# SiLU of the delta heads written through tanh, in three parts, with VectorE multiplying

## The chip, the core and the metric

The kernel runs on one core of a Trainium2 chip. TensorE does the matmuls, VectorE, ScalarE and GpSimd the elementwise work, each engine in the order of its own program; they wait for each other on semaphores. ScalarE computes functions such as Exp, Ln, SiLU or Tanh from a table set that must be loaded first; a load shows in its program as ACT_TABLE_LOAD. The metric is the device time of one execution in microseconds, as a median over runs.

## What is computed

Two blocks of a small transformer over 272 tokens (16 meta tokens and 256 others) of width 1024. The change lies in the first layer, in the mixer that joins a gated delta rule of four heads with a window attention of eight. Of the delta part this matters here:

```python
qkv = jax.nn.silu(centred_conv(jnp.concatenate([hq, hk, hv], axis=-1), conv_w))
q, k, v = split_cols(qkv, (A_QKW, A_QKW, A_VW))          # 512 columns each: 4 heads of 128
q = l2norm(q.reshape(bsz, n, A_HEADS, A_DK)) * (A_DK ** -0.5)
k = l2norm(k.reshape(bsz, n, A_HEADS, A_DK))             # x * rsqrt(sum(x * x) + EPS)
v = v.reshape(bsz, n, A_HEADS, A_DV)
```

silu(x) is x * sigmoid(x), which equals 0.5 * x * (1 + tanh(x / 2)).

## The kernel before

Activations are held with the model's columns on the 128 partitions and the 272 tokens (T) along the free axis. `qkv` is 12 such chunks of 272: queries 0 to 3, keys 4 to 7, values 8 to 11. Weights are split into a high and a low part (`w_hi` by ScalarE at L1771, `w_lo` by VectorE at L2511), so that three matmuls of TensorE (L675) give one product; 24 of them make a tile of the projection.

The stretch in question is one loop of ten steps, k = 0 to 9, that each of the engines runs in its own program. It interleaves three things. First the projection's 16 tiles (`qkvz_tile` on TensorE, `qkvz_step` on VectorE at L2879, which takes a tile from its bank; `next_split` on ScalarE). Second the convolution of the twelve chunks: ScalarE makes products (`conv_products`, L2122), GpSimd the others and the sums (L3592, L3595), and VectorE does chunk 11 alone (`last_conv`, L2850 and L2852); `conv_done` and `conv_last` tell that they are finished. Third the window attention in nine units: TensorE's scores (L1381, L1386), VectorE's bias and maximum (`window_logits`, L2910 to L2925), ScalarE's exponents (`window_exponents`, L2075), VectorE's reciprocal and scaling (`window_normalise`, L2932, L2935), TensorE's transposes (`window_turn`, L1399 to L1403), ScalarE's copies (`window_copies`, L2085 to L2089), TensorE's product with the values (`window_values`, L1412, L1415, and L1421 for unit 8), ScalarE's copy of the result (`window_result`, L2097) and VectorE's low part of it (`window_low`, L2526).

Into the end of this loop the delta heads are woven. In step 6 ScalarE, once the convolution is done, takes the SiLU of all of `qkv` in place (L2156) and then has the table set with logarithm and exponential loaded again (`log_and_exp`, L2011). In step 7 it squares keys and queries (L2150). In step 8 TensorE sums the squares over each head with a matmul by ones (`delta_sum`, L1435), ScalarE takes the logarithm of the sums and the exponential of minus half of it (`delta_logs`, L2108, L2111), and VectorE multiplies the heads by it (`delta_norm`, L2963), keys first, then queries. Behind the loop TensorE transposes values and then keys into token order (`delta_turn`, L1451), ScalarE copies them out (L2163), and the delta rule itself begins (`gated_delta`, L963 and on). GpSimd, when the convolution is done and the projection is read, fills the identity tiles of the delta rule (`identity_tiles`, L3605, L3606).

All orders are written out by hand; each engine's place in the loop is the order of the code in its own program.

Of the kernel before, what the change touches and what calls it, by code (L numbers as in the profile page):

```python
# [25 lines left out]
ALU, ACT, AX = mybir.AluOpType, mybir.ActivationFunctionType, mybir.AxisListType  # L26

P = 128
# [3 lines left out]
T = NMETA + SEQ  # L32
# [174 lines left out]
def program(nc, w, out):  # L207
# [3 lines left out]
    with ExitStack() as ctx:  # L211
# [23 lines left out]
        work = sb("work", [P, 2656])  # L235
# [70 lines left out]
        for d in range(2):  # L306
# [73 lines left out]
        dve_step, act_step, pool_step, out_sent = sem("dve_step"), sem("act_step"), sem("pool_step"), sem("out_sent")  # L380

        M = {n: sem(n) for n in (
            "ab_turned ab_turn_read conv_given conv_done conv_last d_blocks d_copied d_cum d_cum_read d_diff d_dm d_egr d_first d_gate_exp d_gates d_gk d_kdec "
            "d_kn d_kq d_ln d_n d_nn d_o1 d_o d_o_read d_qe d_rows d_s d_s_kept d_s_read d_tiles d_turned d_v d_vnew d_w d_w_copied d_wk "
            "d_wk_copied d_x d_x5 d_x6 d_xt d_y d_yt f_ready f_t f_w f_w_copied f_x f_xt f_y "
            "q_meta sink_meta d_sq d_qsum d_rs d_normed g_ln g_mixed g_n g_read g_sq g_stat gelu kv_dup l_att l_attc l_e1 l_exp l_gate l_ks "
# [100 lines left out]

            return conv_four[:, c // 2 % 2, j - 1] if given_taps(c) == 5 else conv_pair[:, c // 2 % 2]

        KEYS, QUERIES = 0, 1  # L490
        delta_sq = {KEYS: area(work, 0, 4, T), QUERIES: area(mx, 9952, 4, T)}
        delta_r = {KEYS: area(work, 4 * T, 4, T), QUERIES: area(mx, 9952 + 4 * T, 4, T)}
        delta_heads = {KEYS: qkv[:, 4:8], QUERIES: qkv[:, 0:4]}


        PREPARED = CHAINS[0:2] + FIRST + CHAINS[2:]
# [163 lines left out]
        def _(pe):  # L660
# [780 lines left out]
            def delta_turn(i, m, source):  # L1441

                s, e = TILES[m]
                if source == 4:
                    pe.wait_ge(M["d_normed"], 1)
                else:
                    pe.wait_ge(M["d_ln"], 2)
                if i >= 4:
                    pe.wait_ge(M["d_copied"], i - 3)
                for h in range(A_HEADS):  # L1450
                    mm = pe.transpose(tile_bank[i % 4][0:e - s, h * P:(h + 1) * P], qkv[:, source + h, s:e], ident)  # L1451
                mm.then_inc(M["d_turned"], 1)
# [300 lines left out]
        def _(act):  # L1753
# [255 lines left out]
            def log_and_exp():  # L2009

                nc.scalar.preload_act_table_set("natural_log_exp_and_others")  # L2011
# [104 lines left out]
            def conv_products(c):  # L2116
# [6 lines left out]
                                         scale=col("conv", 12 * j + c))  # L2123
                ins.then_inc(M["conv_given"], 1)

            for k in range(WINDOW_UNITS + 1):
                if k == 0:
                    next_split(1)
                if k < 6:
                    conv_products(2 * k)  # L2130
                if k < WINDOW_UNITS:
                    window_exponents(k)
                if k < 6:
                    next_split(2 * k + 2)
                if k == 2:
                    act.wait_ge(M["d_cum_read"], 1)
                    act.activation(necc[0:NMETA, 0], gcc[0:NMETA, 0], ACT.Exp)
                    act.activation(necc[:, 1:3], gcc[:, 1:3], ACT.Exp).then_inc(M["d_gate_exp"], 1)
                if k == 8:
                    delta_logs(KEYS)  # L2140
                if k >= 1:
                    window_result(k - 1)
                if k < 6:
                    next_split(2 * k + 3)
                if k < 5:
                    conv_products(2 * k + 1)
                if k == 7:
                    act.wait_ge(M["silu_done"], 1)
                    for which in (KEYS, QUERIES):
                        act.activation(delta_sq[which], delta_heads[which], ACT.Square).then_inc(M["d_sq"], 1)  # L2150
                if k < WINDOW_UNITS:
                    window_copies(k)
                if k == 6:
                    act.wait_ge(M["conv_done"], 11)
                    act.wait_ge(M["conv_last"], 1)
                    act.activation(qkv, qkv, ACT.Silu).then_inc(M["silu_done"], 1)  # L2156
                    log_and_exp()
                if k == 8:
                    delta_logs(QUERIES)
            for i, (m, source) in enumerate(delta_turns()):  # L2160
                n = TILES[m][1] - TILES[m][0]
                act.wait_ge(M["d_turned"], i + 1)
                act.activation((v_tok if source == 8 else k_tok)[0:n, m], tile_bank[i % 4][0:n, 0:4 * P].rearrange(  # L2163
                    "p (h d) -> p h d", h=4), ACT.Copy).then_inc(M["d_copied"], 1)

            def decays(chain):

# [325 lines left out]
        def _(dve):  # L2493
# [465 lines left out]
            def delta_norm(which):  # L2959

                heads = delta_heads[which].rearrange("p h t -> p (h t)")
                dve.wait_ge(M["d_rs"], which + 1)
                dve.scalar_tensor_tensor(heads, heads, P ** -0.5 if which == QUERIES else 1.0,  # L2963
                                         delta_r[which].rearrange("p h t -> p (h t)"), ALU.mult, ALU.mult)\
                    .then_inc(M["d_normed"], 1)

            dve.wait_ge(M["sink_meta"], 1)
            for k in range(WINDOW_UNITS + 1):
# [17 lines left out]
                    delta_gates()  # L2986
                if k == 5:
                    last_conv()
                if k == 8:
                    delta_norm(QUERIES)  # L2990
            dve.wait_ge(M["d_cum_read"], 1)
# [559 lines left out]
        def _(pool):  # L3551
# [69 lines left out]
                    .then_inc(done, 1)  # L3621

            pool.wait_ge(M["conv_done"], 11)
            pool.wait_ge(tile_read, tile_at[phases["ab_qkvz"].first] + 16)
            for chain in CHAINS:
                identity_tiles(chain)
# [64 lines left out]
```

## Time and profile before

| | us |
|---|---|
| median of three runs | 1565.97 |
| lowest | 1565.91 |
| the profiled execution, whole | 1562.62 |
| its span on the core, first to last instruction | 1560.8 |
| TensorE busy (matmuls) | 1520.3 |
| VectorE busy | 1099.1 |
| ScalarE busy | 798.1 |
| GpSimd busy | 173.7 |

The mean granted clock of TensorE in the profiled execution was 0.994 of its full speed. Times in the rows further down are microseconds from the start of the span. An engine's timeline gives for each merged group of instructions its start, its length, the line, operation, tiles and count, and in brackets how long the engine was idle before it and which instruction ended that. The chain of work that ended last is read from the last instruction backwards, each time to what released it.

### The profile page before, as it was taken

Reading aid. Unit: us, or ns where it says so; the run is one execution under the profiler, and the core shown is the slowest. Engines: PE = TensorE matmul, PEld = TensorE weight load, DVE = VectorE, ACT = ScalarE, POOL = GpSimd, SP = SyncE. Lnnn points to the kernel's source line nnn. Section 1 sums busy time; section 2 is a strip of 40 time slices with the busy share of each in tenths; the row PEclk is TensorE's granted clock in tenths of the full one; section 3 lists DMA queues with packets and bytes.
Section 4 is the critical chain, followed back from the end, with each engine's and each line's share of the span. In section 5 each row is a group of like instructions: output and inputs, shape, how many; then the busy total and the mean of one; then the engine's idle time right before and its main releaser. Section 6 shows DMA issues by size and latency. Waiting matters only on the chain.

```text
span 1560.8 us, 31984 instructions
## 1 busy us (share of the span) xinstructions
PE 1520.3 (97%) x12908; PEld 1471.7 (94%) x12908; DVE 1099.1 (70%) x1965; ACT 798.1 (51%) x1369; POOL 173.7 (11%) x187
## 2 busy tenths in 40 slices
PE   6988999999999999999999999999999999999997
PEld 5977899999998999999998999999999999999997
DVE  5784758676778677778778667776668666666666
ACT  4766445343455544446545655444555556554443
POOL 2481203000021200002000201000010010200000
PEclk9998999999999999999999999999999999999999
DMA  6420016454441345454433424656444444356561
GB/s 223 163 109 1 3 55 213 174 184 180 162 162 68 109 169 208 162 202 176 163 137 134 166 101 141 216 165 209 168 162 163 162 164 161 109 176 202 166 210 58
DMA packets 124791, 236.35 MB, mean 151 GB/s; under 512 B 2614, under 2 KB 50025, under 8 KB 124665
## 3 DMA queue, kind: packets, MB, share of 16 engines
q1 hardware_dynamic: 123177, 230.24, 42.2%
q0 software_dynamic: 1296, 4.28, 0.9%
q8 instruction: 91, 1.49, 0.4%
q14 instruction: 35, 0.29, 0.1%
q10 hardware_dynamic: 192, 0.05, 0.0%
HBM read 233.51 MB, written 1.05 MB: 150 GB/s over the span
## 4 chain that ended last, share of the span: by engine, by line
PE 88%; DVE 6%; ACT 2%; issue 2%; POOL 1%; DMA 0%; ACTq 0%; DVEq 0%; POOLq 0%
PE ps L675 49%; PE ps L722 6%; PE ps L721 6%; PE ps L720 6%; PE ps L683 6%; PE ps L844 2%; DVE w_lo L2511 2%; PE ps L821 1%; PE ps L771 1%; PE ps L806 1%; DVE hidden L2562 1%; PE ps L831 1%; POOL square_sum L3567 0%; DVE chain_memory L3124 0%; ACT w_hi L1771 0%
## 5 line engine op out<-in xcount | busy, mean ns | idle before, releaser
L1771 ACT ACTIVATE w_hi<-raw 128x1024 fp32r<-128x1024 f32 x440 | 460.6, 1051 | 282.1 <-PE ps L722 135.3
L2511 DVE TENSOR_TENSOR w_lo<-raw,w_hi 128x1024 fp32r<-128x1024 f32 x440 | 547.0, 1243 | 9.4 <-ACT w_hi L1771 9.1
L675 PE MATMUL ps<-u_hi,w_hi 128*128 128x256 f32 (+1 forms) x1464 | 422.6, 289 | 1.9 <-issue 1.2
L675 PE MATMUL ps<-u_hi,w_lo 128*128 128x256 f32 (+1 forms) x1464 | 416.8, 285 | 0.0
L675 PE MATMUL ps<-u_lo,w_hi 128*128 128x256 f32 (+1 forms) x1464 | 416.3, 284 | 0.0
L675 PEld LDWEIGHTS ps<-u_hi,w_hi 128*128 128x128 f32 x1464 | 278.0, 190 | 8.0 <-issue 5.6
L675 PEld LDWEIGHTS ps<-u_hi,w_lo 128*128 128x128 f32 x1464 | 278.1, 190 | 0.0
L675 PEld LDWEIGHTS ps<-u_lo,w_hi 128*128 128x128 f32 x1464 | 277.0, 189 | 0.6
L675 PE MATMUL ps<-a_hi,w_hi 128*128 128x256 f32 x800 | 226.7, 283 | 0.6 <-DVE hidden L2562 0.3
L675 PE MATMUL ps<-a_lo,w_hi 128*128 128x256 f32 x800 | 224.9, 281 | 0.0
L675 PE MATMUL ps<-a_hi,w_lo 128*128 128x256 f32 x800 | 224.8, 281 | 0.0
L722 PE MATMUL ps<-a_hi,w_lo 128*128 128x256 f32 (+1 forms) x720 | 204.9, 285 | 0.0
L721 PE MATMUL ps<-a_lo,w_hi 128*128 128x256 f32 (+1 forms) x720 | 204.5, 284 | 0.0
L720 PE MATMUL ps<-a_hi,w_hi 128*128 128x256 f32 (+1 forms) x720 | 204.5, 284 | 0.0
L2562 DVE TENSOR_TENSOR hidden<-ps,hidden 128x256 f32<-128x256 f32 (+1 forms) x272 | 115.7, 425 | 101.7 <-PE ps L722 59.4
L2550 DVE TENSOR_TENSOR work<-ps,rs 128x256 f32<-128x256 f32 (+1 forms) x153 | 65.4, 427 | 133.9 <-PE ps L675 118.0
L675 PEld LDWEIGHTS ps<-a_hi,w_hi 128*128 128x128 f32 x800 | 151.1, 189 | 2.2 <-DVE w_lo L2511 0.8
L675 PEld LDWEIGHTS ps<-a_hi,w_lo 128*128 128x128 f32 x800 | 151.3, 189 | 0.0
L675 PEld LDWEIGHTS ps<-a_lo,w_hi 128*128 128x128 f32 x800 | 150.4, 188 | 0.1
L720 PEld LDWEIGHTS ps<-a_hi,w_hi 128*128 128x128 f32 x720 | 135.8, 189 | 0.2 <-DVE a_lo L2526 0.2
L722 PEld LDWEIGHTS ps<-a_hi,w_lo 128*128 128x128 f32 x720 | 136.0, 189 | 0.0
L721 PEld LDWEIGHTS ps<-a_lo,w_hi 128*128 128x128 f32 x720 | 135.4, 188 | 0.0
(469 smaller groups left out, 2257.1 us busy)
## 6 DMA issues: line engine op xcount, KB each, us to landing
raw<-in_w_ff_dram SPq DMA_DIRECT2D x32, 2048.0 KB, 7.7
raw<-in_ffn_w_gu_dram SPq DMA_DIRECT2D x44, 1024.0 KB, 6.9
raw<-in_ffn_w_down_dram SPq DMA_DIRECT2D x10, 2048.0 KB, 8.0
raw<-in_xa_w_kv_dram SPq DMA_DIRECT2D x8, 2048.0 KB, 8.3
raw<-in_od_w_in_dram SPq DMA_DIRECT2D x6, 2048.0 KB, 7.8
raw<-in_w_in_ab_dram SPq DMA_DIRECT2D x5, 2048.0 KB, 7.9
raw<-in_ev_w_in_dram SPq DMA_DIRECT2D x5, 2048.0 KB, 7.8
raw<-in_xa_w_q_dram SPq DMA_DIRECT2D x4, 2048.0 KB, 7.6
```

Of the source, the lines that this page charges most:

```text
L675: mm = pe.matmul(bank[:, 0:n], wx[:, q, k * P:(k + 1) * P], x[ux][:, k, ts], start=k == 0 and i == 0, stop=k == KD - 1 and i == 2)
L683: mm = pe.matmul(bank[:, at:at + n_quarters * n].rearrange("p (q n) -> p q n", n=n), x[ux][:, k, ts], wx[:, q:q + n_quarters, k * P:k * P ...
L720: pe.matmul(tile_bank[t % 4][:, 0:n], hi[:, k, cols], a[0][:, at_k, ts], start=k == 0, stop=False)
L721: pe.matmul(tile_bank[t % 4][:, 0:n], hi[:, k, cols], a[1][:, at_k, ts], start=False, stop=False)
L722: mm = pe.matmul(tile_bank[t % 4][:, 0:n], lo[:, k, cols], a[0][:, at_k, ts], start=False, stop=k == chunks - 1)
L771: mm = pe.matmul(banks[u_ % 2][:, 0:n], matrix, hn_sq[:, u_ % 2, i * n:(i + 1) * n], start=i == 0, stop=i == tiles - 1)
L806: mm = pe.matmul(bank[:, column:column + matrix.shape[1]], part, matrix, start=i == 0, stop=i == len(parts) - 1)
L844: mm = pe.matmul(bank[x["parts"], r * P:r * P + x["nq"]], vs[r], at_pt[0:rows, v % 2, c, 0:x["nq"]], start=c == 0, stop=c == len(x["keys"] ...
L1771: act.activation(quarter(w_hi, b, q), raw_quarter(b, q), ACT.Copy).then_inc(high_split, 1)
L2511: dve.tensor_tensor(quarter(w_lo, b, q), raw_quarter(b, q), quarter(w_hi, b, q).bitcast(F32), ALU.subtract)\
L2550: dve.tensor_tensor(target, tile_bank[t][:, 0:n], rs[:, ts] if scale is None else scale, ALU.mult)\
L2562: dve.tensor_tensor(hidden[:, k, ts], tile_bank[t][:, 0:ts.stop - ts.start], hidden[:, k, ts], ALU.add)\
```

## The change

The table set that holds Exp and Tanh is loaded ahead of the loop. In step 6 ScalarE takes, in place of the SiLU, tanh(x / 2) of keys, queries and values, in three activations, into areas of their own. VectorE multiplies (tanh + 1) by x, for keys and queries at the end of its step 7, for values in its step 8 between `window_low` and the scaling of the queries; this is twice the SiLU. The squares take 0.5 as scale, the scalings of keys and queries and the copies of the transposed values a factor of 0.5. The squares of keys wait for the first product, those of queries for the second; behind them, and ahead of `window_copies(7)`, stands the load of the set with logarithm and exponential. The transposes on TensorE and the tile filling on GpSimd wait for the third product too.

```diff
--- before.py
+++ after.py
@@ -487,10 +487,11 @@
 
             return conv_four[:, c // 2 % 2, j - 1] if given_taps(c) == 5 else conv_pair[:, c // 2 % 2]
 
-        KEYS, QUERIES = 0, 1
+        KEYS, QUERIES, VALUE_HEADS = 0, 1, 2
         delta_sq = {KEYS: area(work, 0, 4, T), QUERIES: area(mx, 9952, 4, T)}
         delta_r = {KEYS: area(work, 4 * T, 4, T), QUERIES: area(mx, 9952 + 4 * T, 4, T)}
-        delta_heads = {KEYS: qkv[:, 4:8], QUERIES: qkv[:, 0:4]}
+        delta_heads = {KEYS: qkv[:, 4:8], QUERIES: qkv[:, 0:4], VALUE_HEADS: qkv[:, 8:12]}
+        delta_tanh = {KEYS: area(work, 4 * T, 4, T), QUERIES: area(mx, 9952 + 4 * T, 4, T), VALUE_HEADS: area(mx, 9952 + 8 * T, 4, T)}
 
 
         PREPARED = CHAINS[0:2] + FIRST + CHAINS[2:]
@@ -1445,6 +1446,7 @@
                     pe.wait_ge(M["d_normed"], 1)
                 else:
                     pe.wait_ge(M["d_ln"], 2)
+                    pe.wait_ge(M["silu_done"], 3)
                 if i >= 4:
                     pe.wait_ge(M["d_copied"], i - 3)
                 for h in range(A_HEADS):
@@ -2123,6 +2125,7 @@
                                          scale=col("conv", 12 * j + c))
                 ins.then_inc(M["conv_given"], 1)
 
+            nc.scalar.preload_act_table_set("exp_and_others")
             for k in range(WINDOW_UNITS + 1):
                 if k == 0:
                     next_split(1)
@@ -2145,23 +2148,24 @@
                 if k < 5:
                     conv_products(2 * k + 1)
                 if k == 7:
-                    act.wait_ge(M["silu_done"], 1)
                     for which in (KEYS, QUERIES):
-                        act.activation(delta_sq[which], delta_heads[which], ACT.Square).then_inc(M["d_sq"], 1)
+                        act.wait_ge(M["silu_done"], which + 1)
+                        act.activation(delta_sq[which], delta_heads[which], ACT.Square, scale=0.5).then_inc(M["d_sq"], 1)
+                    log_and_exp()
                 if k < WINDOW_UNITS:
                     window_copies(k)
                 if k == 6:
                     act.wait_ge(M["conv_done"], 11)
                     act.wait_ge(M["conv_last"], 1)
-                    act.activation(qkv, qkv, ACT.Silu).then_inc(M["silu_done"], 1)
-                    log_and_exp()
+                    for which in (KEYS, QUERIES, VALUE_HEADS):
+                        act.activation(delta_tanh[which], delta_heads[which], ACT.Tanh, scale=0.5).then_inc(M["delta_tanh"], 1)
                 if k == 8:
                     delta_logs(QUERIES)
             for i, (m, source) in enumerate(delta_turns()):
                 n = TILES[m][1] - TILES[m][0]
                 act.wait_ge(M["d_turned"], i + 1)
                 act.activation((v_tok if source == 8 else k_tok)[0:n, m], tile_bank[i % 4][0:n, 0:4 * P].rearrange(
-                    "p (h d) -> p h d", h=4), ACT.Copy).then_inc(M["d_copied"], 1)
+                    "p (h d) -> p h d", h=4), ACT.Copy, scale=0.5 if source == 8 else 1.0).then_inc(M["d_copied"], 1)
 
             def decays(chain):
 
@@ -2960,9 +2964,15 @@
 
                 heads = delta_heads[which].rearrange("p h t -> p (h t)")
                 dve.wait_ge(M["d_rs"], which + 1)
-                dve.scalar_tensor_tensor(heads, heads, P ** -0.5 if which == QUERIES else 1.0,
+                dve.scalar_tensor_tensor(heads, heads, 0.5 * P ** -0.5 if which == QUERIES else 0.5,
                                          delta_r[which].rearrange("p h t -> p (h t)"), ALU.mult, ALU.mult)\
                     .then_inc(M["d_normed"], 1)
+
+            def double_silu(which):
+
+                dve.wait_ge(M["delta_tanh"], which + 1)
+                dve.scalar_tensor_tensor(delta_heads[which], delta_tanh[which], 1.0, delta_heads[which], ALU.add, ALU.mult)\
+                    .then_inc(M["silu_done"], 1)
 
             dve.wait_ge(M["sink_meta"], 1)
             for k in range(WINDOW_UNITS + 1):
@@ -2986,6 +2996,11 @@
                     delta_gates()
                 if k == 5:
                     last_conv()
+                if k == 7:
+                    double_silu(KEYS)
+                    double_silu(QUERIES)
+                if k == 8:
+                    double_silu(VALUE_HEADS)
                 if k == 8:
                     delta_norm(QUERIES)
             dve.wait_ge(M["d_cum_read"], 1)
@@ -3621,6 +3636,7 @@
                     .then_inc(done, 1)
 
             pool.wait_ge(M["conv_done"], 11)
+            pool.wait_ge(M["silu_done"], 3)
             pool.wait_ge(tile_read, tile_at[phases["ab_qkvz"].first] + 16)
             for chain in CHAINS:
                 identity_tiles(chain)
```

What stands in the engines' programs. On ScalarE, at the place where the loop begins: the last row of the gates is the one at L2066 (L2068 after), then comes the weights' copy for the projection. Before:

```order
L2065 ACTIVATE small<-small 128x24 [waits act_step]
L2066 ACTIVATE small<-small,cst 128x24 [waits act_step]
L1771 ACTIVATE w_hi<-raw 128x1024 [waits tile_summed]
L2122 ACTIVATE mx<-mx,late 128x272 [waits tile_read]
L2075 ACTIVATE att,small<-att,small 128x273 [waits at_max]
```

On ScalarE at the same place, in the changed kernel (L1773 is the weights' copy, L2124 a convolution product, L2077 the exponents of unit 0):

```order
L2067 ACTIVATE small<-small 128x24 [waits act_step]
L2068 ACTIVATE small<-small,cst 128x24 [waits act_step]
L2128 ACT_TABLE_LOAD
L1773 ACTIVATE w_hi<-raw 128x1024 [waits tile_summed]
L2124 ACTIVATE mx<-mx,late 128x272 [waits tile_read]
L2077 ACTIVATE att,small<-att,small 128x273 [waits at_max]
```

One load more stands there, ahead of everything of the loop.

On ScalarE in steps 6 to 8, from the copies of window unit 6 to the logarithms of the keys (`ps` are the banks, `att` the window's probabilities, `mx` and `work` hold the heads). Before:

```order
L2086 ACTIVATE att<-ps 32x128
L2156 ACT_TABLE_LOAD [waits conv_last]
L2156 ACTIVATE mx<-mx 128x3264 [waits conv_done]
L2011 ACT_TABLE_LOAD
L2075 ACTIVATE att,small<-att,small 128x273 [waits at_prob,at_max]
L2097 ACTIVATE a_hi<-ps 128x128 [waits at_summed]
L2150 ACTIVATE work<-mx 128x1088 [waits silu_done]
L2150 ACTIVATE mx<-mx 128x1088
L2085 ACTIVATE att<-ps 128x512 [waits at_summed,at_turned]
L2108 ACTIVATE work<-ps,cst 128x272 [waits d_qsum]
```

The same stretch of ScalarE in the changed kernel:

```order
L2088 ACTIVATE att<-ps 32x128
L2161 ACTIVATE work<-mx 128x1088 [waits conv_last,conv_done]
L2161 ACTIVATE mx<-mx 128x1088 x2
L2077 ACTIVATE att,small<-att,small 128x273 [waits at_prob,at_max]
L2099 ACTIVATE a_hi<-ps 128x128 [waits at_summed]
L2153 ACTIVATE work<-mx 128x1088 [waits silu_done]
L2153 ACTIVATE mx<-mx 128x1088 [waits silu_done]
L2013 ACT_TABLE_LOAD
L2087 ACTIVATE att<-ps 128x512 [waits at_summed,at_turned]
L2110 ACTIVATE work<-ps,cst 128x272 [waits d_qsum]
```

The two loads around the SiLU are gone, three tanh stand in its place, both squares wait for VectorE, and a load stands between them and the copies of unit 7.

On VectorE in steps 7 and 8, from the tile 15 of the projection (L2879, L2883 after) to the scaling of the queries (L2963, L2967 after). Before:

```order
L2879 TENSOR_TENSOR mx<-ps,rs 128x272 [waits tile_summed]
L2932 RECIPROCAL small<-small 128x2 [waits at_exp]
L2526 TENSOR_TENSOR a_lo<-ps,a_hi 128x128 [waits operand_high]
L2918 COPY att<-small 128x1 [waits at_turned]
L2925 TENSOR_REDUCE small<-att 128x1 [waits at_biased]
L2963 SCALAR_TENSOR_TENSOR mx<-mx,work 128x1088 [waits d_rs]
L2963 SCALAR_TENSOR_TENSOR mx<-mx 128x1088 [waits d_rs]
```

The same stretch of VectorE in the changed kernel:

```order
L2883 TENSOR_TENSOR mx<-ps,rs 128x272 [waits tile_summed]
L2936 RECIPROCAL small<-small 128x2 [waits at_exp]
L2530 TENSOR_TENSOR a_lo<-ps,a_hi 128x128 [waits operand_high]
L2974 SCALAR_TENSOR_TENSOR mx<-work,mx 128x1088 [waits delta_tanh]
L2974 SCALAR_TENSOR_TENSOR mx<-mx 128x1088 [waits delta_tanh]
L2922 COPY att<-small 128x1 [waits at_turned]
L2929 TENSOR_REDUCE small<-att 128x1 [waits at_biased]
L2967 SCALAR_TENSOR_TENSOR mx<-mx,work 128x1088 [waits d_rs]
L2974 SCALAR_TENSOR_TENSOR mx<-mx 128x1088 [waits delta_tanh]
L2967 SCALAR_TENSOR_TENSOR mx<-mx 128x1088 [waits d_rs]
```

Three multiplications (L2974) have come in: two ahead of the logits of unit 8, one ahead of the scaling of the queries.

## Rows read from the trace of the kernel before

**Rows 1.** The page: span, and the engines' shares of the chain that ended last.
```profile
span 1560.8 us, 31984 instructions
...
PE 88%; DVE 6%; ACT 2%; issue 2%; POOL 1%; DMA 0%; ACTq 0%; DVEq 0%; POOLq 0%
```

**Rows 2.** Timeline of ScalarE where the loop begins (start, length, instruction, idle before).
```profile
55.85 1.04 ACT L1771 ACTIVATE w_hi<-raw 128x1024 fp32r<-128x1024 f32 x1
...
57.63 0.51 ACT L2075 ACTIVATE att<-att,small 128x273 f32<-128x273 f32 x1
```

**Rows 3.** Timeline of VectorE in the same stretch.
```profile
58.97 1.15 DVE L2935 TENSOR_SCALAR att<-att,small 128x272 f32<-128x272 f32 x2
```

**Rows 4.** Timeline of TensorE in the same stretch.
```profile
60.01 0.29 PE L675 MATMUL ps<-u_hi,w_lo 128*128 128x272 f32 x1
60.17 0.66 PE L1399 MATMUL ps<-cst,att 128*128 128x128 f32 x4
```

**Rows 5.** Timeline of GpSimd: its first and its last convolution work.
```profile
57.81 0.71 POOL L3592 TENSOR_TENSOR mx<-mx,late 128x272 f32<-128x272 f32 x1 [28.44 <-ACT mx L2122]
...
104.20 10.60 POOL L3595 TENSOR_TENSOR mx<-mx 128x272 f32<-128x272 f32 x10
```

**Rows 6.** The chain in order of time, 60 to 180 us (start, length, what).
```profile
92.94 3.23 PE ps L675 x24
...
114.29 0.95 DVE att L2935 x2
115.28 1.12 PE ps L1399 x4
```

**Rows 7.** Timeline of ScalarE, steps 6 to 8.
```profile
117.41 1.28 ACT L2156 ACT_TABLE_LOAD   x1
118.71 2.93 ACT L2156 ACTIVATE mx<-mx 128x3264 f32<-128x3264 f32 x1
121.65 1.28 ACT L2011 ACT_TABLE_LOAD   x1
122.95 0.52 ACT L2075 ACTIVATE att<-att,small 128x273 f32<-128x273 f32 x1
...
125.14 1.09 ACT L2150 ACTIVATE mx<-mx 128x1088 f32<-128x1088 f32 x1
126.50 0.60 ACT L2085 ACTIVATE att<-ps 128x512 f32<-128x512 f32 x1 [0.27 <-PE ps L1400]
...
130.55 1.62 ACT L2108 ACTIVATE work<-ps,cst 128x272 f32<-128x272 f32 x4 [1.82 <-PE ps L1435]
132.21 1.11 ACT L2111 ACTIVATE work<-work 128x1088 f32<-128x1088 f32 x1
```

**Rows 8.** Timeline of VectorE, steps 7 and 8.
```profile
122.39 0.44 DVE L2879 TENSOR_TENSOR mx<-ps,rs 128x272 f32<-128x272 f32 x1 [2.98 <-PE ps L675]
124.10 0.17 DVE L2932 RECIPROCAL small<-small 128x2 f32<-128x2 f32 x1 [1.27 <-ACT att L2075]
124.30 1.33 DVE L2935 TENSOR_SCALAR att<-att,small 128x272 f32<-128x272 f32 x2
125.56 0.28 DVE L2526 TENSOR_TENSOR a_lo<-ps,a_hi 128x128 fp32r<-128x128 f32 x1
...
133.35 1.29 DVE L2963 SCALAR_TENSOR_TENSOR mx<-mx,work 128x1088 f32<-128x1088 f32 x1 [4.02 <-ACT work L2111]
134.56 0.28 DVE L2526 TENSOR_TENSOR a_lo<-ps,a_hi 128x128 fp32r<-128x128 f32 x1
```

**Rows 9.** Timeline of TensorE: sums of the squared keys, window unit 8.
```profile
127.00 3.52 PE L1435 MATMUL ps<-work,cst 128*128 128x272 f32 x8
...
134.99 2.34 PE L1421 MATMUL ps<-att,mx 16*64 16x32 f32 x24 [0.66 <-DVE a_lo L2526]
```

**Rows 10.** Windows: busy PE, PEld, DVE, ACT, POOL, then PEclk, DMA share, GB/s.
```profile
34.00:36.00 2.00, 1.34 (x9) 1.27 (x10) 0.80 (x1) 1.47 (x5) 0.00 (x0) 1.00 1.04 398
...
128.00:130.00 2.00, 2.00 (x6) 1.35 (x4) 0.61 (x3) 0.61 (x2) 0.00 (x0) 0.50 0.00 0
```

## What I expect of the change, and why

> **What bounds the kernel now.** I read the page's chain of work first: TensorE holds 88% of it in a span of 1560.8 us [rows 1]. The change touches only about 55 to 140 us, so I went to the chain in order of time and to the timelines of single engines there. Between 60 and 96 us the chain is TensorE's projection matmuls (the last piece before it changes hands is at 92.94) [rows 6]. After it the window attention and the convolutions run on ScalarE and VectorE; at 114.29 VectorE normalises the probabilities of unit 6, and TensorE, which stood idle, starts again at 115.28 [rows 6]. From there to 140 us hardly anything overlaps: the chain is a relay. ScalarE loads a table at 117.41, runs the one SiLU at 118.71 for 2.93 us, loads the next table at 121.65 and only at 122.95 gets to the exponents of unit 7 [rows 7]. VectorE normalises them at 124.30 [rows 8]; TensorE sums the squares of the keys from 127.00 [rows 9]; ScalarE takes logarithms at 130.55 and the exponential at 132.21 [rows 7]; VectorE scales the keys at 133.35 and splits unit 7's result at 134.56 [rows 8]; this releases TensorE at 134.99 [rows 9]. Transposes and the delta rule follow. So I forecast by how much 134.99 moves. Behind it all is either relay or TensorE's own work (its 88% of the chain), without slack in which a shift could vanish; I carry it to the end one for one.
>
> **First part: the table load ahead of the window loop.** The new load is the first thing behind the Ln at L2066, so it stands in front of ScalarE's copy of a weight quarter at 55.85, of the first convolution products and of the exponents of unit 0 at 57.63 [rows 2]. All loads of the trace are alike: the one at 121.65 takes 1.28 us, and what follows it starts 1.30 us after it [rows 7]. Neither row lists idle time ahead of it, so ScalarE runs without a gap here [rows 2] and all of it moves by 1.28. Who waits? VectorE's normalising at 58.97 follows the exponents and lasts 1.15, to 60.12 [rows 3]. TensorE's last matmul before it needs these probabilities starts at 60.01, its neighbours are 0.13 apart, and the transposes start at 60.17 [rows 4]. The slack is therefore at most 0.05 us, and TensorE loses about 1.25 us here. I take 1.25. It could be less only if TensorE caught up before 96 us, and there it is the chain itself. A second carrier gives the same: GpSimd gets its first convolution product at 57.81 and then works through to 114.80 (the last ten additions start at 104.20 and last 10.60) [rows 5], so it too ends 1.28 later. That end alone would cost nothing: 116.08 is before 117.41, when the activation behind it could start. An idle stretch of this length doesn't slow TensorE's clock by itself: from 34 to 36 us it was busy 1.34 of 2.00 us at clock 1.00 [rows 10].
>
> **Second part: SiLU replaced by tanh.** Three tanh of 128x1088 take the place of load, SiLU, load. No tanh stands in the trace. From below: the SiLU did 3264 columns in 2.93 us; from above: a single 1088 column activation takes 1.09 (the square at 125.14) [rows 7], so three are 2.93 to 3.27. I take 3.05, nearest to the SiLU, since instructions of one engine overlap at their ends. They start at 117.41 + 1.25 = 118.66, and exponents of unit 7 start at 121.7 instead of 122.95, and end at 122.85 (they took 1.1 us before VectorE went on at 124.10 [rows 8]). So 2.57 us of loads left the place, 1.25 came in early, 0.1 is lost to three instructions: 1.2 us earlier. But VectorE has an earlier duty in its program: it must evacuate projection tile 15, which it did at 122.39 on TensorE's release, in 0.44 us [rows 8]. TensorE is 1.25 late: 123.64, done at 124.08. So the reciprocal of unit 7 stays at about 124.1, where it was. **The gain from the removed loads ends here**: of 1.2 us nothing is left, and tanh has 1.2 us of cover (0.4 each) before it counts.
>
> **Third part: two multiplications and a load in the relay.** The normalising of unit 7 took 1.33 us while GpSimd filled tiles; GpSimd now waits for the third product, so I take the 0.95 of unit 6 [rows 6] and 0.05 around it: from 124.25 to 125.25. The split of window unit 6 (0.28, at 125.56 before [rows 8]) ends at 125.5. Now the new instructions. A multiplication is taken as VectorE's scaling of keys, same operation and shape: 1.29, of which 1.21 until the next starts [rows 8]. Bounds: 1.21 and, with a disturbance as the normalising had, 1.7. Keys 125.45 to 126.7, queries to 127.9. ScalarE squares the keys behind the first (in cover), the queries behind the second, 127.95 to 129.05 (1.09 [rows 7]); then the table load, to 130.3; then what the load was put in front of: the copies of window unit 7, which stood at 126.50 and take 0.60 and a short one [rows 7], to about 131.0; then exponents of unit 8, which are one head, half of the 1.1 above: 131.65. Only then the logarithms of the keys, at 131.7; before, 130.55. TensorE's sum of squared keys starts at 127.8 instead of 127.00 and takes 3.52 at worst [rows 9], to 131.3, so it is no longer the last to arrive. From 131.7 on the relay is the old one: **+1.15 us** on the keys' scaling, the split and TensorE's 134.99.
>
> The rest is in cover. The values' multiplication stands behind the split on VectorE, 135.9 to 137.1, when VectorE formerly waited for the queries' exponential; TensorE needs it only for the transposes of the values, after the 2.3 us of work that 134.99 begins. The squares, with scale 0.5, and the rescaled copies cost what they did. GpSimd's tile filling moves behind the third product, to about 137 us; the delta rule, which reads the tiles, comes behind the transposes.
>
> **A rule against the trace.** The row at 121.65 shows a load that starts when the SiLU ends and is followed by the exponents without a gap [rows 7]. The Trainium skill, ScalarE: Activation LUTs, section What ACT_TABLE_LOAD costs, counts a switch of sets as about 1283 ns of load and about 1380 ns in which the engine drains, 2.66 us in all. The load agrees with this trace; the drain doesn't show in it, so by the row a switch is 1.3.
>
> **Sum.** +1.25 carried in by the first load, -1.3 gained and lost again at tile 15, +1.2 from the third part: relay at 134.99 later by 1.15, say +1.1. Span 1560.8 + 1.1 = 1561.9. The profiled execution took 1562.62; the median of the three times is 1565.97, 3.35 above it, so the median goes to 1567.1.
>
> **Rivals.**
> *The first load is hidden* (TensorE and GpSimd catch up before 115 us, or the exponents of unit 0 were not what it waited for). Then tile 15 comes at 122.39, exponents of unit 7 end at 121.6, and everything of the third part is 1.25 earlier: -0.1 us, 1565.9. For it: both slacks were read from modelled matmul ends. Against: the chain names TensorE without a break up to 96 us [rows 6]. 0.12.
> *TensorE's clock falls less often.* The sums of the keys ran partly at half clock (0.50 from 128 to 130 us) [rows 10], 3.52 us for what at full clock would be no less than half, 1.8. The stretch idle before them becomes shorter. The sums themselves are in cover now, so only work after 134.99 could gain, by perhaps 1.5 us: -0.4, 1565.6. 0.10.
> *Slower: the clock falls once more.* The pause of 1.25 us at 60 us, or a differently cut relay after 125 us, puts a stretch at half clock that wasn't. Price: sums of 3.52 against 1.8 are up to 1.7 us [rows 9]; one or two such stretches on the path give +2.5 to +4.5, 1569. It decides once TensorE shows a clock of 0.50 in a stretch that stood at 1.00 before and that its successor waits for. For it: clock 0.50 [rows 10] in this very place. Against: 1.00 around the pause at 34 us [rows 10]. 0.13.
> *A switch costs more than its row*, twice 1.28: the load ahead of the loop and the one behind the squares both stand on the path, +1.15 + 2.56 = +3.7, 1569.7. Against: the row shows no gap [rows 7]. 0.04. This is the skill's drain, named above; by its figure it would be +3.9.
> *Tanh is slower than 0.4 us above its peers*: +1 to +3. 0.03.
>
> **Chances and range.** Forecast 0.58, its own range 1566 to 1568.5. All cases lie between 1565 and 1570; single executions of before differ by 3.4 us between profile and median, so I open the range to 1562.5 and 1571. A measurement of this kernel can tell some 2%, 31 us, from no change; no mechanism here has a tenth of that. Faster 0.01, within 2% 0.98, slower 0.01.
>
> **What would show it.** Right: the load ahead of the loop lasts 1.28 and TensorE's transposes of unit 0 start near 61.4, waiting for VectorE; tile 15 releases VectorE near 123.6; the reciprocal of unit 7 stays near 124.1; logarithms of the keys near 131.7 follow the exponents of unit 8 at once; the work of 134.99 stands near 136.1. Wrong: transposes of unit 0 at 60.2, or logarithms of the keys waiting for TensorE, or a multiplication over 1.5 us.

## The result, and the profile after

Over 17 executions the changed kernel took 1569.76 us in the median (1565.72 to 1571.66), the kernel before 1564.42 in as many. One execution of the kernel before, a slow one of 1651.88 us, is left out of the ratio. The ratio is 1.0026, with a 95% interval of 1.0018 to 1.0033: some 4 us longer (3 to 5; the medians differ by 5.3), far within 2%. The profiled execution has a span of 1564.1 us against 1560.8 [rows 1], at the same mean clock of 0.994. With 1565.94 us it is one of the fastest five of the changed kernel, so its trace shows 3.3 us and not the whole of a usual execution. The forecast of no visible change, +1.1 us, had the right sign, and less than half of the size.

The traces show four shifts, not one. First the places that the forecast named. ScalarE where the loop begins (start, length, instruction, idle before and what ended it):

```profile
57.87 0.32 ACT L2068 ACTIVATE small<-small,cst 128x24 f32<-128x24 f32 x1
58.20 1.28 ACT L2128 ACT_TABLE_LOAD   x1
59.49 1.06 ACT L1773 ACTIVATE w_hi<-raw 128x1024 fp32r<-128x1024 f32 x1
...
61.28 0.51 ACT L2077 ACTIVATE att<-att,small 128x273 f32<-128x273 f32 x1
```

TensorE of the same kernel, transposes of window unit 0:

```profile
63.76 0.44 PE L1400 MATMUL ps<-cst,att 128*128 128x128 f32 x2 [1.23 <-DVE att L2939]
```

The load takes 1.28 us, and TensorE, which did not idle here before [rows 4], now waits 1.23 us for VectorE. But the weights' copy starts at 59.49, and before it started at 55.85 [rows 2]: 3.64 later, of which the load explains 1.3. Something had already come 2.2 us late before the loop. It is in ScalarE's timeline further ahead. Before:

```profile
40.19 1.06 ACT L1771 ACTIVATE w_hi<-raw 128x1024 fp32r<-128x1024 f32 x1 [3.82 <-DMA raw<-in_w_in_ab_dram]
```

After:

```profile
42.43 1.06 ACT L1773 ACTIVATE w_hi<-raw 128x1024 fp32r<-128x1024 f32 x1 [6.22 <-DMA raw<-in_w_in_ab_dram]
```

A block of projection weights lands 2.24 us later, in a part of the program that the change does not touch.

The relay, ScalarE after, which answers to [rows 7]:

```profile
120.88 1.09 ACT L2161 ACTIVATE work<-mx 128x1088 f32<-128x1088 f32 x1
121.88 2.09 ACT L2161 ACTIVATE mx<-mx 128x1088 f32<-128x1088 f32 x2
123.88 0.51 ACT L2077 ACTIVATE att<-att,small 128x273 f32<-128x273 f32 x1
...
129.90 1.11 ACT L2153 ACTIVATE mx<-mx 128x1088 f32<-128x1088 f32 x1
131.02 1.28 ACT L2013 ACT_TABLE_LOAD   x1
132.32 0.60 ACT L2087 ACTIVATE att<-ps 128x512 f32<-128x512 f32 x1
...
132.97 0.51 ACT L2077 ACTIVATE att<-att,small 128x273 f32<-128x273 f32 x1
...
133.47 1.57 ACT L2110 ACTIVATE work<-ps,cst 128x272 f32<-128x272 f32 x4
```

VectorE after, which answers to [rows 8]:

```profile
125.85 0.44 DVE L2883 TENSOR_TENSOR mx<-ps,rs 128x272 f32<-128x272 f32 x1 [2.86 <-PE ps L676]
126.21 0.15 DVE L2936 RECIPROCAL small<-small 128x2 f32<-128x2 f32 x1
126.40 0.63 DVE L2939 TENSOR_SCALAR att<-att,small 128x272 f32<-128x272 f32 x2
127.17 0.29 DVE L2530 TENSOR_TENSOR a_lo<-ps,a_hi 128x128 fp32r<-128x128 f32 x1
127.38 1.28 DVE L2974 SCALAR_TENSOR_TENSOR mx<-work,mx 128x1088 f32<-128x1088 f32 x1
128.58 1.28 DVE L2974 SCALAR_TENSOR_TENSOR mx<-mx 128x1088 f32<-128x1088 f32 x1
```

TensorE after, which answers to [rows 6] and [rows 9]:

```profile
118.86 1.11 PE L1400 MATMUL ps<-cst,att 128*128 128x128 f32 x4 [5.04 <-DVE att L2939]
...
129.95 2.07 PE L1436 MATMUL ps<-work,cst 128*128 128x272 f32 x8 [1.49 <-ACT work L2153]
...
137.86 2.34 PE L1422 MATMUL ps<-att,mx 16*64 16x32 f32 x24 [0.66 <-DVE a_lo L2530]
140.13 2.79 PE L1453 MATMUL ps<-cst,mx 128*16 128x128 f32 x24
143.79 2.05 PE L964 MATMUL ps<-cst,small 128*128 128x128 f32 x16 [0.88 <-ACT mx L2167]
```

Against before: the transposes of unit 6 are 3.58 later (118.86 for 115.28), the product of unit 8 is 2.87 later (137.86 for 134.99), so the relay itself became 0.71 us shorter. The logarithms follow the exponents of unit 8 with no idle time. Then the clock enters. Before, the transposes of the heads ran in part at half clock; TensorE's rows of before:

```profile
137.26 4.46 PE L1451 MATMUL ps<-cst,mx 128*16 128x128 f32 x24
142.43 2.05 PE L963 MATMUL ps<-cst,small 128*128 128x128 f32 x16 [0.72 <-ACT mx L2163]
```

They took 4.46 us, and 2.79 after; the delta rule starts only 1.36 later than before. This gain is lost again some 45 us later, where the windows of the changed kernel (busy PE, PEld, DVE, ACT, POOL, then granted clock, DMA share, GB/s) show a fall of the clock to 0.50; before it stood at 1.00 in the same work:

```profile
188.00:190.00 2.00, 1.28 (x25) 1.15 (x20) 1.65 (x4) 0.38 (x1) 0.00 (x0) 0.72 0.00 0
190.00:192.00 2.00, 2.00 (x35) 2.00 (x35) 0.29 (x1) 0.66 (x3) 0.00 (x0) 0.50 0.03 8
```

The sum by TensorE's rows: +2.24 (block) +1.34 (load) -0.71 (relay) -1.51 (transposes at full clock) +1.68 (up to 225.03 for 221.99, nearly all of it the fall at 189) = +3.04; the rest up to +3.3 comes in behind.

### The profile page after: what moved, and what is told of

The parts are those of the page before. It is cut to its first block, busy times and chain, and to the rows that moved or that the text cites. A ratio compares the mean times of both kernels' runs of the same rounds, so it can differ in the third digit from the quotient of the medians.

```text
span 1564.1 us, 31992 instructions
## 1 busy us (share of the span) xinstructions
PE 1520.7 (97%) x12908; PEld 1472.4 (94%) x12908; DVE 1102.1 (70%) x1968; ACT 797.1 (51%) x1371; POOL 174.3 (11%) x187
## 4 chain that ended last, share of the span: by engine, by line
PE 87%; DVE 7%; ACT 2%; issue 2%; DMA 1%; POOL 1%; ACTq 0%; DVEq 0%; POOLq 0%
PE ps L676 48%; PE ps L723 6%; PE ps L722 6%; PE ps L721 6%; PE ps L684 6%; PE ps L845 2%; DVE w_lo L2515 2%; PE ps L822 1%; PE ps L772 1%; DMA raw<-in_w_in_ab_dram 1%; PE ps L807 1%; DVE hidden L2566 1%; PE ps L832 1%; POOL square_sum L3582 0%; DVE chain_memory L3139 0%
## 5 line engine op out<-in xcount | busy, mean ns | idle before, releaser
L1773 ACT ACTIVATE w_hi<-raw 128x1024 fp32r<-128x1024 f32 x440 | 460.5, 1051 | 283.6 <-PE ps L723 135.3
```

The source lines that it names most:

```text
L1773: act.activation(quarter(w_hi, b, q), raw_quarter(b, q), ACT.Copy).then_inc(high_split, 1)
```

## The experiments

Each ran beside the kernel before. In their texts, theories A and B are about the clock; C and E came up as the runs were read.

**r1.** The kernel before, unchanged.

> The kernel before, unchanged, timed against itself, to see how far executions scatter and what clock goes with them. Theory A (the change costs about 1.3 us of loads ahead of the loop and 0.6 us in the relay, the rest of the measured 4 us are stretches at half clock that the new order brings more often): executions of before cluster at a mean clock near 0.994, with few below. Rival B (the clock falls are chance and as frequent before): clocks of 0.990 to 0.992 are as common here as in the changed kernel (there 12 of 17), and ratio 1.000 with an interval of some 0.001.

Measured 1564.54 us (1563.91 to 1568.23), ratio 1.0003 [0.9994, 1.0012]. Mean clocks of the eleven executions lay between 0.990 and 0.992, their mean was 0.991; of the changed kernel it was 0.992. So theory A's half on the clock falls, as far as the mean clock tells: the changed kernel does not lose more of it. At equal clock it is longer: executions at 0.994 took 1565.7 to 1566.5, and the profiled one of before took 1562.62 at 0.994. The block landed at 40.26, so 40.19 was no accident.

**r2.** The load ahead of the loop alone.

```diff
+            nc.scalar.preload_act_table_set("exp_and_others")
             for k in range(WINDOW_UNITS + 1):
                 if k == 0:
                     next_split(1)
```

> The kernel before with one edit: the table load that the change puts ahead of the window loop. Theory A: TensorE's transposes of window unit 0 wait about 1.2 us for VectorE, everything behind is later by 1.25 to 1.35, the relay from 117 to 135 us keeps its lengths, and the time is +1.3 us (ratio 1.0008). Rival (hidden): no wait, ratio 1.0000. If the pause or the shift itself brings clock falls, +3 us or more with a mean clock of 0.990 to 0.992.

Measured 1569.96 us (only five executions), ratio 1.0043 [1.0029, 1.0057], not less than the whole change. TensorE of this kernel:

```profile
65.19 0.66 PE L1399 MATMUL ps<-cst,att 128*128 128x128 f32 x4 [1.22 <-DVE att L2936]
```

The wait is the forecast one, 1.22. But ScalarE's copy of the block starts at 42.37 here too, and a stretch at half clock follows the pause (0.50 from 46 to 48 us): the last activation ahead of the load starts at 59.30, 3.7 later than the same one before, at 55.63. The load costs 1.3; the other part stands ahead of it. Of these 3.7 us the late block makes 2.2 and the fall 1.5: this last activation starts 16.93 us after the block's copy, and 15.44 in the kernel before and in the trace of the changed kernel, whose clock stays at 1.00 here.

**r3 and r4.** The changed kernel with loads moved into ScalarE's idle time. r3 moves the first:

```diff
-            nc.scalar.preload_act_table_set("exp_and_others")
...
+                if k == 6:
+                    nc.scalar.preload_act_table_set("exp_and_others")
                 if k < WINDOW_UNITS:
                     window_exponents(k)
```

r4 moves the second as well:

```diff
                 if k < WINDOW_UNITS:
                     window_exponents(k)
+                if k == 7:
+                    log_and_exp()
...
                         act.activation(delta_sq[which], delta_heads[which], ACT.Square, scale=0.5).then_inc(M["d_sq"], 1)
-                    log_and_exp()
```

> The changed kernel with the load of the Exp and Tanh set moved from ahead of the loop to ahead of the exponents of window unit 6, where ScalarE is idle for 6.2 us. Theory A: the load is free there, TensorE's transposes of unit 0 no longer wait, and the time is 1.3 us below the changed kernel, so about the kernel before plus what the clock adds. If the pause at 60 us brought the clock falls, the mean clock goes back to 0.994 and the time to within 1 us of before or below.

> The changed kernel with both loads moved: the first ahead of the exponents of unit 6, the second from behind the squares to behind the exponents of unit 7, where ScalarE is idle for 1.9 us. Theory A: beyond the 1.3 us of the first move, copies of unit 7 start 1.3 us earlier, the logarithms of the keys then wait for TensorE's sums (to 132.0 in the changed kernel against 133.5), so 1.1 us more: 2.4 below the changed kernel, 1.3 to 2 below before by length of work. The clock can add or take 1.5 to 4.

Measured 1567.94 us (r3), ratio 1.0019 [1.0009, 1.0029], and 1569.14 us (r4), 1.0024 [1.0014, 1.0034]. Neither came down to before. The loads themselves were free, as expected: TensorE has no wait at unit 0 in either trace. But the copy of the block started at 43.84 and 43.12, and as in r2 the clock then falls to 0.50 from 46 to 48 us, which adds 1.4 to 1.5 us more. r4's relay shows the second move; its ScalarE:

```profile
131.28 0.58 ACT L2087 ACTIVATE att<-ps 128x512 f32<-128x512 f32 x1
...
134.00 1.62 ACT L2110 ACTIVATE work<-ps,cst 128x272 f32<-128x272 f32 x4 [1.50 <-PE ps L1436]
```

Now the logarithms wait 1.50 us for TensorE's sums, which ran at half clock here (3.66 us). From the transposes of unit 6 (119.69) to the product of unit 8 (138.44) it is 18.75 us, against 19.00 in the changed kernel and 19.71 before (19.37 in r1). With the sums at full clock, in r12, it is 18.29: 0.7 below the changed kernel, where I had expected 1.1 from this move.

**r5.** The same load in a place where nobody can feel it: the kernel before with the load ahead of the exponents of unit 6, in 6.2 us of idle time.

```diff
+                if k == 6:
+                    nc.scalar.preload_act_table_set("exp_and_others")
                 if k < WINDOW_UNITS:
                     window_exponents(k)
```

> The kernel before with one edit that its critical path can't feel: the load of the Exp and Tanh set stands ahead of the exponents of window unit 6, where ScalarE was idle for 6.2 us. Theory C (new, from the four traces: in every changed program the small strided weight load that GpSimd issues at 28.4 us lands 3.7 to 4.9 us later than before, and the 2 MB block of projection weights behind it at 42.4 to 43.8 instead of 40.2; what changed is the program itself, not the place of any work up to then): the block lands at 42 us or later again, TensorE idles some 2 us at 43, and the time is 2 to 4 us above before. Rival D (the landing has to do with the load ahead of the loop or with tanh): landing at 40.2, time within 0.5 us of before.

Measured 1568.39 us, ratio 1.0020 [1.0011, 1.0029]. ScalarE of r5:

```profile
43.24 1.06 ACT L1771 ACTIVATE w_hi<-raw 128x1024 fp32r<-128x1024 f32 x1 [6.61 <-DMA raw<-in_w_in_ab_dram]
```

A program with one instruction more, 70 us further on, waits 2.8 us longer for this block and is 1.7 to 4.5 us slower. The late landing needs neither tanh nor the load ahead of the loop; theory C holds and rival D falls. It doesn't need the new semaphore `delta_tanh` either, an edit of the change that the diff at the top leaves out: r2 and r5 have none. As in r2 to r4, the pause is followed by a fall of the clock, here in r5:

```profile
46.00:48.00 2.00, 2.00 (x10) 2.00 (x10) 1.98 (x4) 1.53 (x4) 0.00 (x0) 0.50 0.72 263
```

The last activation of the gates starts at 60.19 for 55.63: 3.05 us by the block and 1.5 by the fall. TensorE's pause before it was 2.53 us here, and 1.96 in r2. In the trace of the changed kernel, with 2.14, and in the nine traces in which the block costs TensorE no pause, the clock is 1.00 there. What is slow shows in the DMA view of 26 to 46 us (tensor, queue, count, KB, us from issue to landing). Before:

```profile
small<-in_od_w_g_dram POOLq DMA_DIRECT2D x1, 64.0 KB, 5.0
small<-in_a_log_dram POOLq DMA_DIRECT2D x1, 4.0 KB, 3.7
small<-in_dt_bias_dram POOLq DMA_DIRECT2D x1, 4.0 KB, 3.4
small<-in_b_sink_dram POOLq DMA_DIRECT2D x1, 4.0 KB, 3.5
```

r5:

```profile
small<-in_od_w_g_dram POOLq DMA_DIRECT2D x1, 64.0 KB, 9.3
small<-in_a_log_dram POOLq DMA_DIRECT2D x1, 4.0 KB, 3.8
small<-in_dt_bias_dram POOLq DMA_DIRECT2D x1, 4.0 KB, 5.2
small<-in_b_sink_dram POOLq DMA_DIRECT2D x1, 4.0 KB, 5.5
```

The last three are vectors of 32 bytes that all 128 partitions read from the same place; two of them land 1.8 and 2.0 us later than before, and the strided weight load in the first row, which is issued behind them, 4.3 us later. While they land, the queues are busy and hardly move anything. The windows at that time, before and then of the changed kernel:

```profile
30.00:32.00 2.00, 2.00 (x18) 2.00 (x17) 2.00 (x4) 1.06 (x1) 0.00 (x0) 1.00 1.08 76
```

```profile
30.00:32.00 2.00, 2.00 (x19) 2.00 (x18) 2.00 (x3) 1.06 (x1) 0.00 (x0) 1.00 0.81 10
```

SyncE issues the 2 MB block at 29.8, into this.

**r6 to r8.** The strided weight load (`wg1`, 64 KB in pieces of 64 bytes) issued behind the delta rule; r6 is the kernel before with it, r7 the changed kernel, r8 that with both table loads moved.

```diff
-            misc(wg1, w["od_w_g1_2"][0].rearrange("(k p) r -> p k r", p=P))
...
+            later(wg1, w["od_w_g1_2"][0].rearrange("(k p) r -> p k r", p=P))
```

> The kernel before with the small strided weight load (64 KB in pieces of 64 bytes, used only in the second layer) issued by GpSimd behind the delta rule instead of at 28.4 us. Theory C: it took its share of the queues that the 2 MB block needs; without it the block lands at 40.2 or earlier, and the time is equal to before or up to 1 us below. It's the reference for the next two.

> The changed kernel with the small strided weight load issued behind the delta rule. Theory C: the block lands near 40.2 also here, so 2.2 us of the shift ahead of the loop go, and the difference to the same kernel without the change is what the change itself costs: 1.3 for the load ahead of the loop and 0.6 less in the relay with the clock's share, +1.0 to +2.5 us. Rival: the landing stays at 42.4 and the difference to before stays near 4 us.

> The changed kernel with both table loads in ScalarE's idle time and the small strided load issued behind the delta rule. Theory C: block at 40.2, no wait at unit 0, logarithms of the keys 1.1 us earlier than in the changed kernel: 1.5 to 2.5 us below the same reference without the change, so near 1562 us, unless the clock falls more often (mean clock under 0.991).

Measured 1564.21, 1566.28 and 1561.74 us, ratios 0.9999 [0.9990, 1.0008], 1.0007 [0.9998, 1.0015] and 0.9986 [0.9974, 0.9997]. The block's copy started at 38.59 in r6 but at 40.45 in r7 and 40.28 in r8: 1.6 to 2.8 earlier than with the strided load in its place, and still 1.7 to 1.9 apart. So theory C had a cause, not the cause: the strided load adds its part, but the broadcast vectors are slower in r7 too (5.4 and 6.6 us to landing, against 3.4 and 4.4 in r6). At 40.4 the block is just early enough (r7's last activation ahead of the load starts at 55.89 and not at 57.87), so the loss is hidden, and the two kernels differ by 2.1 us in the median, 0.9 in the mean.

**r9 to r12.** The other four small loads moved too, onto SyncE's queue at 18 us, where nothing moves. r9 is the kernel before with this, r10 that with the load ahead of the loop, r11 the changed kernel, r12 that with both table loads moved.

```diff
+            def small_loads():
+                sp.wait_ge(sum_added, 1)
+                misc(early[:, 0:ew], w["early_tables"])
+                misc(a_log, w["a_log"].rearrange("o d h -> (o d h)").partition_broadcast(P))
+                misc(dt_bias, w["dt_bias"].rearrange("o d h -> (o d h)").partition_broadcast(P))
+                misc(sink, w["b_sink"].rearrange("o h -> (o h)").partition_broadcast(P))
```

> The kernel before with GpSimd's four small loads (tables, and three vectors that every partition reads from the same few bytes) issued on SyncE's queue at about 18 us, where the queues move nothing, instead of at 26 us; the strided weight load stays behind the delta rule. Theory E (from the traces: between 30 and 32 us all queues are busy and move 76 GB/s before, 10 to 37 in every changed program, while those vectors land; the 2 MB block is issued into this at 29.8): with them gone the block lands at 38.6 or earlier, PE doesn't wait for it, and the time is that of before or up to 0.5 us below. It is the reference for the other three.

> As the reference of this call, with the table load ahead of the window loop added and nothing else of the change. Theory E: the block lands where it does in the reference, within 0.3 us, and the load alone costs 1.25 to 1.35 us ahead of TensorE's transposes of unit 0, plus what the clock makes of it: +1.3 to +2.5 us in time. If the landing differs by 2 us again, the broadcast vectors are not what makes it late.

> The changed kernel with the small loads as in the reference of this call. Theory E: the landing is as in the reference; the difference is what the change costs by itself: +1.3 for the load, -0.6 to -0.7 in the relay up to the start of unit 8's product, sum +0.6 to +0.7, and the clock: +0.5 to +2 us. My forecast for this step was +1.1. Rival: +4 us as measured with the small loads in their old place.

> The changed kernel with both table loads in ScalarE's idle time and the small loads as in the reference. Theory E: 2 to 3 us below the reference (relay shorter by 1.9 by the traces: -1.3 for the load, -1.1 behind the squares against the changed kernel), so about 1562 us or below; with little clock loss 1560.

| | median us | ratio to before | block copied at | transposes, unit 0 | product, unit 8 |
|---|---|---|---|---|---|
| r9 (before) | 1564.10 | 0.9998 [0.9989, 1.0008] | 38.63 | 60.11 | 134.92 |
| r10 (load only) | 1567.10 | 1.0011 [0.9998, 1.0025] | 38.66 | 61.45 | 136.27 |
| r11 (change) | 1565.70 | 1.0007 [0.9995, 1.0019] | 38.57 | 61.53 | 135.62 |
| r12 (change, loads moved) | 1563.71 | 0.9986 [0.9974, 0.9998] | 40.07 | 61.22 | 134.62 |

The block's copy starts within 0.1 us in r9 to r11, and with it the 2.2 us are gone from the change. These runs move the tables and the three vectors together; which of the four matters is not separated. (All of r12's trace runs 1.1 us late from the beginning, its weights' copy ahead of the block starts at 34.28 for 33.17; that is not the change.) The traces now give the change in pure form: the load ahead of the loop +1.34 at unit 0 and +1.35 at unit 8 (r10), the whole change +0.70 at unit 8 (r11), so the relay is 0.65 shorter than with the load alone. In time r11 is 1.6 us above r9 by the medians and 0.7 by the means of twelve runs each. Resampling these runs, the difference of means is 0.7 with 95% between -0.4 and +1.7; for r10 it is 1.6 (0.0 to 2.8), for r12 -1.8 (-3.2 to -0.5).

TensorE of r11, where the relay and the sums show the changed kernel's rows again, 2 us earlier:

```profile
61.53 0.66 PE L1412 MATMUL ps<-cst,att 128*128 128x128 f32 x4 [1.22 <-DVE att L2952]
```

ScalarE of r12, the best order: the load behind the exponents of unit 7 lies in idle time, copies, exponents and logarithms follow the squares at once.

```profile
122.47 1.28 ACT L2025 ACT_TABLE_LOAD   x1
...
128.02 1.11 ACT L2168 ACTIVATE mx<-mx 128x1088 f32<-128x1088 f32 x1
129.04 0.58 ACT L2099 ACTIVATE att<-ps 128x512 f32<-128x512 f32 x1
...
130.18 1.62 ACT L2122 ACTIVATE work<-ps,cst 128x272 f32<-128x272 f32 x4
```

r8 and r12 are the versions that beat both kernels: 0.9986 of before, some 2 us, with both intervals below 1, but hardly. The gain comes with the clock, whose mean is 0.994 and 0.993 there and 0.992 before. At equal clock little is left: at 0.992 five executions of r12 took 1564.2 us in the mean, and eleven of the kernel before, timed beside them, 1564.5.

## Why the prediction was right, and where its size was off

The time lies within the stated range (1562.5 to 1571), and the forecast case, no visible change with a small loss, is what came. That the time lies inside is in part luck: the range was opened for scatter, and 1569.76 is above the forecast's own 1566 to 1568.5, by a cause that the forecast doesn't have. Its level of 1567.1 also stood on a median of three, 1565.97, where seventeen executions give 1564.42. Two rivals named nearly this time, 1569 and 1569.7, but by other mechanisms (below). The steps:

- **The load ahead of the loop, +1.25.** Right: 1.28 us of load, 1.22 to 1.23 us of wait on TensorE, +1.34 at unit 0 (r10). The slack was nil, and the TensorE that is the chain up to 96 us carried it on undiminished to 115 us. The first rival, that it is hidden, is excluded by r10.
- **Three tanh for load, SiLU, load.** Right: 121.88 to 123.88 for the last two, each 1.0 us until the next instruction, 3.0 in all for my 3.05. Tanh costs what its peers cost.
- **The gain ends at tile 15.** Right: the exponents of unit 7 were ready by 125.0, but VectorE took tile 15 at 125.85 and went on to the reciprocal at 126.21 with no idle time between. Nothing of the removed loads came through here.
- **The relay behind it, forecast 1.15 later at the product of unit 8, measured 0.70 (r11).** Between the transposes of unit 6 and this product the forecast took off 0.1 us, and the traces took off 0.71 (19.71 to 19.00). Of these 0.6 us the normalising of unit 7 makes the largest part: from its start to the first multiplication it is 0.98 us and not 1.20. The step itself I took as 0.95 from unit 6's row, and it took 0.63 (1.33 before). What I used as the undisturbed price was itself taken while GpSimd still worked on its last addition (until 114.80 [rows 5]). In the seven traces in which GpSimd waits for the third product it takes 0.63 or 0.64, and in the seven in which GpSimd fills tiles beside it 0.78 to 1.33 (0.78 in r1), so the gain against before is 0.15 to 0.7. Another 0.18 lies ahead of its start, where tile 15 came 0.12 earlier behind the transposes than I forecast, and 0.18 at the copies and the exponents of unit 8. The multiplications (1.28, by my 1.29), the squares, the load and the order of arrival, logarithms right behind the exponents of unit 8, were as forecast.
- **The clock.** The second rival came in part: sums and transposes at full clock, -1.5 us. The third too: a new fall at 189 us, +1.5. In this trace they cancel, and r11 shows both again (0.50 from 188 to 190). Over the runs the mean clocks of both kernels are alike, 0.992. What the forecast didn't see is the fall at 46 us behind the late block, 1.4 to 1.5 us in each of r2 to r5.
- **A switch costs more than its row.** This rival is excluded for this kernel, though its 1569.7 is what was measured: in the changed kernel the weights' copy starts 1.29 us after the load at 58.20, and r10 prices one more switch on the path at 1.34, not at 2.6. The Trainium skill's drain (ScalarE: Activation LUTs, What ACT_TABLE_LOAD costs) doesn't show in these rows either.
- **The step that was missing.** This is where the forecast's size failed: "the change touches only about 55 to 140 us". I compared only the stretch that the change touches and took all of the program up to 55 us as unchanged. It wasn't: the block of projection weights came 2.2 us later. r5 shows that it comes late with one harmless instruction more; r9 to r11 show that with the small loads out of its way the change costs what its own steps cost. 4 us measured are about 1 of the change and about 3 of this, by medians and means that carry 1 us of scatter each. The trace of the changed kernel has 2.2 us of the late block; r2 has 3.7, with the fall of the clock behind it. How many of the seventeen executions had that fall is not shown, since only one of the fastest was profiled.

What stays open is why the broadcast loads are slower in the longer programs. Their place in the program, the instructions before them and their times of issue are the same to 0.3 us. They are slower too when SyncE issues them early (4.5 and 4.9 us in r11 for 3.5 and 4.0 in r9), where it harms nobody. The place of tensors or of the program in memory would be a possible cause; no run here tests it.

## What to carry to other kernels

Price a moved table load by the place where it is put, and look for idle time of its engine on either side: both loads of this change cost 1.3 and about 0.7 us where they stand and nothing 50 us later or 6 us earlier. A gain ahead of an engine with another duty in its program order is worth nothing until that duty moves too. When two programs are compared at the level of some microseconds, first lay the traces beside each other in the stretch that was not edited, and put the same edit where nobody can feel it: here that control was as slow as the change.

## What was not expected of the hardware

Loads in which all 128 partitions read the same 32 bytes take 3.4 to 5.5 us for 4 KB (6.6 in r7), and while two or three of them land the queues are 0.8 to 1.1 busy and move 76 GB/s or only 10, where the block of weights gets 373 to 410 later. Without the strided load among them the changed kernel (r7) moves 5 GB/s there at 0.85 busy. Their duration changes by 1.8 to 2.0 us with a program that differs by one table load 70 us later. A pause of TensorE of 2.14 us at 43 us left the clock at 1.00 in the trace of the changed kernel, and pauses of 1.96 to 3.15 us there were followed by 0.50 in the four of r2 to r5. And VectorE's scaling of 128x272, twice, took 0.63 us alone, 0.95 with GpSimd at its end and 0.78 to 1.33 with GpSimd filling tiles beside it.
